# Start of a fused trunk kernel: the first two gate/up pairs come in five contraction parts, the next two in unused SBUF

## The reference

```python
def rms_norm(x, w, eps=NORM_EPS):
    y = xf * lax.rsqrt(jnp.mean(xf * xf, axis=-1, keepdims=True) + eps)
    return (y * w.astype(jnp.float32)).astype(x.dtype)

def swiglu(x, w_gate, w_up, w_down):
    return (jax.nn.silu(x @ w_gate) * (x @ w_up)) @ w_down

h = h + 0.5 * swiglu(rms_norm(h, norm_ff1[i]), ffn1_gate[i], ffn1_up[i], ffn1_down[i])
```

## Time and profile before

| | us |
|---|---|
| median of 3 runs (lowest to highest) | 1050.06 (1049.46 to 1050.34) |
| span of the profiled execution | 1048.1 |
| PE busy in it | 1039.2 (99%) |
| DVE busy | 804.6 (77%) |
| ACT busy | 616.0 (59%) |
| POOL busy | 51.0 (5%) |
| q1 (SP's DMA queue) | 188.79 MB, 63.7% of the 16 engines |

### The profile page before, as it was taken

One profiled execution on the slowest core, in us unless ns is written; L12 is line 12 of the kernel. 1 busy time (PEld: TensorE's weight loads), 2 busy tenths in 40 slices (PEclk: granted clock), 3 DMA queues, 4 the chain that ended last, 5 costly groups with the idle time before them and its releaser, 6 DMA issues.

```text
span 1048.1 us, 18314 instructions
## 1 busy us (share of the span) xinstructions
PE 1039.2 (99%) x6542; PEld 931.7 (89%) x6542; DVE 804.6 (77%) x1192; ACT 616.0 (59%) x979; POOL 51.0 (5%) x70
## 2 busy tenths in 40 slices
PE   9999999999999999999999999999999999999997
PEld 8888888999999988888888888888998998888886
DVE  7888777699768888887766888776689678888663
ACT  7655554478878775555435556543456766556441
POOL 0200012100000000000111000011100000000021
PEclk9999999999999999999999999999999999999999
DMA  9966766559545566666865666676555456667671
GB/s 261 225 189 193 210 195 177 161 152 276 137 120 160 167 197 196 187 195 173 221 182 159 191 193 189 188 219 175 150 166 167 121 156 197 191 192 205 178 205 40
DMA packets 363298, 190.12 MB, mean 181 GB/s; under 512 B 6080, under 2 KB 360672, under 8 KB 363248
## 3 DMA queue, kind: packets, MB, share of 16 engines
q1 hardware_dynamic: 362848, 188.79, 63.7%
q0 software_dynamic: 256, 0.59, 0.3%
q10 hardware_dynamic: 144, 0.10, 0.1%
HBM read 187.86 MB, written 1.07 MB: 180 GB/s over the span
## 4 chain that ended last, share of the span: by engine, by line
PE 95%; DVE 2%; ACT 1%; SPq 1%; issue 1%; DMA 0%; DVEq 0%; ACTq 0%
PE psum L259 46%; PE psum L265 24%; PE psum L240 6%; PE psum L244 6%; PE psum L241 6%; PE psum L1809 1%; PE psum L1814 1%; PE psum L1737 1%; DMA raw<-in_ffn_gate 0%; PE psum L1080 0%; SPq L194 0%; PE psum L1097 0%; DVE xn L355 0%; PE psum L1098 0%; DVE arena L1510 0%
## 5 line engine op out<-in xcount | busy, mean ns | idle before, releaser
L229 DVE TENSOR_TENSOR wlo<-raw,whi 128x1024 fp32r<-128x1024 f32 (+1 forms) x322 | 414.9, 1307 | 68.6 <-ACT whi L224 67.4
L224 ACT ACTIVATE whi<-raw 128x1024 fp32r<-128x1024 f32 (+1 forms) x322 | 351.7, 1113 | 22.7 <-PE psum L244 20.0
L259 PE MATMUL psum<-xn,whi 128*128 128x512 f32 x1392 | 350.4, 393 | 0.4 <-DVE xn L355 0.2
L259 PEld LDWEIGHTS psum<-xn,whi 128*128 128x128 f32 x1392 | 250.6, 189 | 46.2 <-DVE xn L355 1.0
L265 PEld LDWEIGHTS psum<-xn,wlo 128*128 128x128 f32 x1392 | 190.2, 190 | 13.7
L265 PE MATMUL psum<-xn,wlo 128*128 128x256 f32 x1392 | 194.6, 282 | 0.0
L259 PE MATMUL psum<-hid,whi 128*128 128x512 f32 x704 | 171.8, 391 | 0.0
L259 PEld LDWEIGHTS psum<-hid,whi 128*128 128x128 f32 x704 | 128.1, 189 | 24.0
L240 PE MATMUL psum<-xn,whi 128*128 128x256 f32 x416 | 104.5, 289 | 0.0
L241 PE MATMUL psum<-xn,whi 128*128 128x256 f32 x416 | 101.9, 283 | 0.0
L265 PEld LDWEIGHTS psum<-hid,wlo 128*128 128x128 f32 x704 | 92.9, 191 | 4.9
(11 more groups left out here) (248 smaller groups left out, 940.2 us busy)
## 6 DMA issues: line engine op xcount, KB each, us to landing
raw<-in_ffn_down SPq DMA_DIRECT2D x64, 704.0 KB, 4.6
raw<-in_ffn_gate SPq DMA_DIRECT2D x87, 512.0 KB, 3.8
raw<-in_ffn_up SPq DMA_DIRECT2D x87, 512.0 KB, 3.9
raw<-in_hyb_w_in SPq DMA_DIRECT2D x36, 512.0 KB, 4.8
raw<-in_dif_w_qkv SPq DMA_DIRECT2D x24, 512.0 KB, 4.3
raw<-in_hyb_w_out SPq DMA_DIRECT2D x16, 512.0 KB, 4.2
raw<-in_dif_w_o SPq DMA_DIRECT2D x8, 512.0 KB, 3.7
hid<-cs_rows SPq DMA_DIRECT2D x4, 512.0 KB, 7.1
```

Of the source, the lines that this page charges most:

```text
L224: act.activation(whi[:, s, 0:k * P], raw[:, s, 0:k * P], ACT.Copy).then_inc(s_whi, 1)
L229: dve.tensor_tensor(wlo[:, s, 0:k * P], raw[:, s, 0:k * P], whi[:, s, 0:k * P].bitcast(F32), ALU.subtract).then_inc(s_wlo, 1)
L259: mm = pe.matmul(acc, hi[:, j, :], x[:, t, :, :], start=start and j == 0, stop=own and stop and j == k - 1)
```

## The change

The program's first stage is rebuilt; all later stages keep their instructions.

- `PARTS` become (0,1), (1,2), (2,4), (4,6), (6,8) tiles, and each part now holds the tiles of all four blocks 0 to 3 (pairs 0 and 1), as DMAs of one tile of two blocks (128 KB): two per tile, 16 in all.
- SP issues `xT` for the first two parts only; ACT issues the other three itself, behind its first square root.
- Blocks 4 to 7 go to an unused stretch of `arena` (`staged`, four slots) and are split from there; the ring's first loads are blocks 8 to 11, which wait until the last part is split.
- `first_pairs` multiplies each part for all four blocks; in the last part blocks 0 and 1 are finished before blocks 2 and 3. `zero_products` remains twice ahead of part 0, `WARM` becomes 4.
- Pair 2 gets PSUM banks 6 and 7 (`third_parts`). `token_sums` stands behind pair 2 (it stood between the two blocks of pair 1). Pair 3 waits for `s_gu` 2. The PE loop starts with pair 4, and there it waits for `s_gu` 3, which is `merge` of pair 2.
- ACT: squares, splits and corrections of blocks 4 to 7 interleaved, then `token_rms`, then silu and `hidden_hi` of pairs 0 and 1, then the loop with `split_hi` of block 8.
- DVE: `staged_lo(0)`, `merge` of pair 0, `staged_lo(1)`, `merge` of pair 1, two `input_sums`, `staged_lo(2)`, two `input_sums`, `staged_lo(3)`, `token_scale`, the two `normalize`, `product` and `hidden_lo` of both pairs, then `step(2, 0)` with block 8 and `merge` of pair 2.

```diff
-WARM = 5
-PARTS = ((0, 2), (2, 4), (4, 6), (6, 7), (7, 8))
+WARM = 4
+PARTS = ((0, 1), (1, 2), (2, 4), (4, 6), (6, 8))
+STAGED = 9216
+            if isinstance(b, int) and b < 3 * RING:
+                sp.wait_ge(s_wlo, RING)
+            for k in range(k0, k1):
+                for s, w in enumerate((gate, up)):
+                    dst = raw[:, s:RING:2, k * P:(k + 1) * P]
+                    src = w[k * P:(k + 1) * P, 0:2 * P].rearrange("p (b m) -> p b m", b=2)
+                    sp.dma_start(dst, src).then_inc(s_part[i], 16)
+        def staged_hi(act, s):
+            act.wait_ge(s_blk, s + 1)
+            act.wait_ge(s_staged[s], 16)
+            act.activation(whi[:, s, 0:SLOT_IN], staged(s), ACT.Copy).then_inc(s_whi, 1)
+        def staged_lo(dve, s):
+            dve.wait_ge(s_whi, RING + s + 1)
+            dve.tensor_tensor(wlo[:, s, 0:SLOT_IN], staged(s), whi[:, s, 0:SLOT_IN].bitcast(F32),
+                              ALU.subtract).then_inc(s_wlo, 1)
...
@@ ffn_sync, n == 0
-                    load_x(sp, i, k0, k1)
+                    if i < X_BY_SYNC:
+                        load_x(sp, i, k0, k1)
                     load_part(sp, i, gate, up)
-                for s, w in ((2, gate), (3, up)):
-                    load(sp, s, s, w[:, P:2 * P].rearrange("(k p) m -> p k m", p=P), DT)
-                sp.dma_start(con[:, 0:P], a["con"][:, 0:P]).then_inc(s_ones, 16)
-                gate_up(1, True)
+                for s in range(RING):
+                    load_staged(sp, s, (gate, up)[s % 2], 2 * P + (s // 2) * P)
+                    if s == 1:
+                        sp.dma_start(con[:, 0:P], a["con"][:, 0:P]).then_inc(s_ones, 16)
+                gate_up(2)
...
@@ ffn_tensor, n == 0
+                    if i < LAST:
+                        pe.wait_ge(s_phi, i + 1)
+                        rounded(range(RING), tiles)
+                        pe.wait_ge(s_plo, i + 1)
+                        rests(range(RING), tiles)
+                    else:
+                        pe.wait_ge(s_whi, RING)
+                        rounded(range(0, 2), tiles)
+                        pe.wait_ge(s_wlo, RING)
+                        rests(range(0, 2), tiles)
+                        rounded(range(2, RING), tiles)
+                        rests(range(2, RING), tiles)
...
-                first_pair()
-                zero_products(5)
-                gate_up(p0 + 1, 1, before_up=lambda: token_sums(pe, n))
-            with pe.Fori(1, FT // 2) as it:
+                first_pairs()
+                gate_up(p0 + 2, 0, acc=(banks[6], banks[7]))
+                token_sums(pe, n)
+                pe.wait_ge(s_gu, 2)
+                gate_up(p0 + 3, 1)
+            with pe.Fori(1 if n else 2, FT // 2) as it:
...
@@ ffn_scalar, n == 0
+                input_squares(act, 0)
+                input_squares(act, 2)
+                staged_hi(act, 0)
+                corrections(p0, 0)
+                staged_hi(act, 1)
+                corrections(p0 + 1, 1)
+                input_squares(act, 4)
+                input_squares(act, 6)
+                staged_hi(act, 2)
+                staged_hi(act, 3)
                 token_rms(act, n)
+                for g in range(2):
+                    silu(hb + g, g)
+                    hidden_hi(hb + g, g, g)
...
@@ ffn_vector, n == 0
+                staged_lo(dve, 0)
+                merge(p0, hb, 0, True)
+                staged_lo(dve, 1)
+                merge(p0 + 1, hb + 1, 1, True)
                 input_sums(dve, 0)
                 input_sums(dve, 1)
+                staged_lo(dve, 2)
                 input_sums(dve, 2)
                 input_sums(dve, 3)
+                staged_lo(dve, 3)
                 token_scale(dve, n)
+                for g in range(2):
+                    normalize(hb + g, g)
+                for g in range(2):
+                    product(hb + g, g)
+                    hidden_lo(hb + g, g, g)
+                step(2, 0, third_parts)
+                step(2, 1)
...
@@ scalar block, start
+            for i in range(X_BY_SYNC, len(PARTS)):
+                load_x(act, i, *PARTS[i])
```

More of the change, by code:

```diff
@@ L120, in trunk @@
         s_raw = [sem(f"s_raw{i}") for i in range(RING)]
-        s_part = [sem(f"s_part{i}") for i in range(len(PARTS) - 1)]
+        s_staged = [sem(f"s_staged{i}") for i in range(RING)]
+        s_part = [sem(f"s_part{i}") for i in range(len(PARTS))]
         s_dhi = sem("s_dhi")
@@ L175, in tile_of, with load @@
             return buf[:, s, 0:k * P].rearrange("p (k m) -> p k m", k=k)
[L177 to L179 removed]
+        def load(sp, b, s, src, k):
+            if isinstance(b, int) and b < 3 * RING:
+                sp.wait_ge(s_wlo, RING)
+            else:
                 sp.wait_ge(s_wlo, b - RING + 1)
@@ L217, in load_x, with split_hi @@
             sp.dma_start(h[:, tiles, :], a["xT"].rearrange("(d p) t -> p d t", p=P)[:, tiles, :]).then_inc(s_x[i], 16)
[L219 to L223, removed]
+        def split_hi(act, b, s, k, turn):
+            act.wait_ge(s_blk, b - RING + 1)
+            act.wait_ge(s_raw[s], turn * 16 - 16)
             act.activation(whi[:, s, 0:k * P], raw[:, s, 0:k * P], ACT.Copy).then_inc(s_whi, 1)
@@ L554, in zero_products, with first_pairs, rounded, rests @@
                     pe.matmul(banks[7][:, 0:P], rb[:, 0:P], rb[:, 0:P], start=True, stop=True)
-            def first_pair():
-                hi, lo = (part.rearrange("p s (k m) -> p s k m", k=DT) for part in (whi[:, 0:2, 0:SLOT_IN], wlo[:, 0:2, 0:SLOT_IN]))
+            def first_pairs():
+                hi, lo = (buf[:, 0:RING, 0:SLOT_IN].rearrange("p s (k m) -> p s k m", k=DT) for buf in (whi, wlo))
+                def rounded(blocks, tiles):
+                    for b in blocks:
+                        for t in tiles:
+                            pe.wait_ge(s_xlo, t + 1)
+                            pe.matmul(wide(b // 2, b % 2), hi[:, b, t, :], xn[:, t, :, :], start=t == 0, stop=False)
+                def rests(blocks, tiles):
+                    for b in blocks:
+                        for t in tiles:
+                            mm = pe.matmul(wide(b // 2, b % 2)[:, T:2 * T], lo[:, b, t, :], xn[:, t, 0, :], start=False,
+                                           stop=t == DT - 1)
+                        if t == DT - 1:
+                            mm.then_inc(s_blk, 1)
                 for i, (k0, k1) in enumerate(PARTS):
@@ L561, in first_pair @@
                     if i == 0:
[L562 to L565, removed]
+                        pe.wait_ge(s_xhi, 1)
                         zero_products(2)
[L567 to L579, removed]
+                    if i < LAST:
[3 more added lines that the diff above has]
+                        rests(range(RING), tiles)
+                    else:
+                        pe.wait_ge(s_whi, RING)
[4 more added lines that the diff above has]
+                        rests(range(2, RING), tiles)
             if n:
@@ L679, in ffn_vector, with merge @@
             p0, hb = first[n], hidden_before(n)
-            def merge(p, q, g, early=False):
+            def merge(p, q, g, early=False, parts=wide_parts):
                 dve.wait_ge(s_blk, p * 2 + 2)
@@ L686, in merge @@
                 dve.wait_ge(s_cor, q + 1)
-                dve.tensor_tensor(gu[:, g, :, :], wide_parts(g)[0], cor[:, g, :, :], ALU.add).then_inc(s_gu, 1)
+                dve.tensor_tensor(gu[:, g, :, :], parts(g)[0], cor[:, g, :, :], ALU.add).then_inc(s_gu, 1)
             def normalize(q, g):
```

86 lines of the change are left out of this document (30 added, 56 removed).

## The result

| | before | changed |
|---|---|---|
| median (lowest to highest), 4 launches each | 1050.2 (1049.46 to 1050.5) | 1055.92 (1054.19 to 1057.54) |
| ratio, 95% interval | | 1.0057 (1.0045 to 1.0069) |
| span of the profiled execution | 1048.1 | 1052.1 |

The change makes the kernel slower by 5.7 us, where 3.1 was forecast. (Before has four launches here, three in the table ahead of the prediction.) The launches of the changed kernel lie 3.4 us apart, those of before 1.0. Five more launches of it (first experiment) gave 1054.28 in the middle, so its loss is 4.3 to 5.7 us, depending on the set of launches; the middle of all nine is 1055.44.

The account below looks back on a forecast made before the run. PE was taken as the bound; at pair 4, PE alone -0.8, sums wait +1.3, merge wait +2.5, start from idle +0.1 gave a 3.1 us loss. 1050.06 + 3.1 = 1053.2 us, range 1051.2 to 1055.2.

Parts of the forecast that it names:

- The bound and the mechanism: At the start, PE gains by block 3, then waits for DVE and ACT; pair 4 starts at 34.8 against 31.68.
- the sums: PE before the token sums: ready at 24.9, it idles 1.3 us until the last input sums end at 26.2.
- the merge: PE before pair 4: idle 2.5 us until the merge of pair 2 ends at 34.7.
- part 2 as landed once 2.20 MB have passed: Input loading: at the rates seen before, part 2 lands at 9.7 us and PE has it at 10.8.
- the upper bound of 10.75: Latest landing of part 2, when before's last part landed behind the same 2.20 MB; carries through to 1054.3 us.
- an order kinder to SP: Input loading: SP's queue served ahead of ACT's would bring part 2 earlier than 9.7, at 8.4 at the earliest.
- the chain of DVE and ACT: From block 0's end at 17.85: 8.3 us to the token sums; from their end 7.9 to pair 2's merge at 34.7.
- rival (c): TensorE's clock falls in the gaps between parts and the later ones, costing 2 us: 1055.2 us; chance 0.12.
- the table load: Silu table load on ACT after the root, 1.28 us: costed at nothing, over 0.6 us before normalize.
- the loads of blocks 4 to 11: Blocks 4 to 7 land by 20 us and cost nothing; ring loads issue near 16, block 8 not wanted before 31.
- (a): Part 2 at 8.4 to 9 and a chain shorter by half a microsecond or more: loss 0.5 to 2 us, about 1051.5; chance 0.18.
- (b): DVE and ACT do not hold PE at pair 4; PE's own sum decides: 1049.3 us, down to 1047.3; chance 0.06.

Follow-up runs that it names:

- first experiment: The changed kernel launched five more times with no edit: 1054.28 us (1054.16 to 1055.5).
- The experiment with the early sums: Changed kernel with squares and sums ahead of block 4's split, token sums ahead of pair 2, token scale and silu worked in earlier: 1051.61 us.
- the one with the removed wait: Changed kernel with pair 4 not waiting for the merge of pair 2, pair 5 still waiting for that of pair 3: 1054.33 us.
- the kernel with the hold: Changed kernel with SP waiting for part 2 to land before it issues part 3, launched twice: 1057.97 and 1056.36 us.
- the second trace: Profiled launch of the changed kernel run again with no edit: 1055.44 us, span 1053.4.
- the kernel with filled parts: Changed kernel with products of zeros put back: 6 instead of 4 at the start, 3 behind part 0 and 3 behind part 1: 1055.98 us.
- the first trace: Profiled launch of the changed kernel from its first four launches, no further edit: 1054.19 us, span 1052.1.
- both kernels with the late gaps filled: Unread products, 3 before the token sums and 8 before pair 4, in the changed kernel: 1054.28 us; also with all input issued by SP: 1054.3.

## Why the prediction was right and where it was wrong

**The bound and the mechanism: right.** All of the loss sits at pair 4, and PE has its two new waits where they were put: 1.1 us for the sums (1.3 forecast) and 2.5 us for the merge (2.5). Counted from block 3's end the merge of pair 2 ends 15.5 us later (35.44 - 19.92); forecast was 15.4 (34.7 - 19.3). The experiment with the early sums took the chain's part away and with it 2.6 us; the one with the removed wait showed that the wait only passes the chain on.

**The data: the term that was mis-sized.** The step "part 2 as landed once 2.20 MB have passed", 9.7, failed. With the input on two queues it landed at 10.2 to 10.8 in six traces and at 11.5 to 11.6 in two, and the upper bound of 10.75, taken from before's last part, was too low. The runs show two things in its place. Bytes that passed are not a DMA that is complete: 98% had passed at 9.0, the last one was done at 10.2 (the kernel with the hold). And it matters that ACT issues part of the input: with one queue part 2 was copied at 9.6 to 10.1, with two at 10.3 to 11.6. I had counted the second issuer as neutral for bandwidth and allowed only for an order kinder to SP; the order was worse for it, for part 0 above all (0.5 to 2.3 us later). How much of this is the mixing and how much the 0.52 MB less ahead of part 2 is open. This term is worth 0.6 us in the profiled launch and 1.9 in one like the second trace.

**The landing term by launches.** Put into the forecast's own sum, part 2 ready at 11.39 to 12.7 instead of 10.8 gives pair 4 at 35.4 to 36.7 and a time of 1053.8 to 1055.1. Measured at pair 4: 35.57 to 36.88. The other 0.2 us in both is the chain of DVE and ACT, 0.1 us longer than forecast (17.0 against 16.9 from block 0's end), and rounding. The range of the data was taken from one trace and used as the range of the launches. The landing alone thus brings a launch to the end of the range: that of the second trace took 1055.44, 0.2 beyond it.

**The clock, rival (c): partly right.** It was priced at 2 us and put between the parts as much as in the late gaps. In the parts the half level did occur (part 0 of the profiled launch; granted clock 0.50 from 8 to 10 us in the second trace) but beside a wait for data, and filling these gaps did not help. Behind the 2.5 us gap it cost 1.3 us in one trace and 1.5 in two, and nothing in three, among them the change's own two. By the Trainium skill ("TensorE: Matmul & The Clock Gate", "Part 1: The HAM clock gate") idleness takes the full clock back. The three traces with a loss agree; the other three kept the full clock over the same gap. For the change itself a fallen clock behind the gap is argued and not shown. The 3.4 us between its four launches are more than the 1.3 us that late data alone made between its two traces. Their mean granted clocks fit only roughly: 0.998, 0.995, 0.997 and 0.995 at 1054.19, 1057.54, 1055.98 and 1055.87 us. Only the fastest of the four has a trace.

**The range** ended at 1055.2, the value of rival (c) alone. Late data (part 2 copied at 11.51) and a fallen clock (1.3 us) did come in the same launch, that of the kernel with filled parts, which took 1056.66. I had let the cases exclude each other. Luck has a part in the miss as well: the middle of the first four launches, 1055.92, lies outside the range, that of the next five, 1054.28, inside.

**Costed at nothing, and rightly:** the table load (over 0.65 us early), the removed fillers (1050.06 against 1050.0 in the kernel before), and the loads of blocks 4 to 11. Rivals (a) and (b), a small loss and a gain, had no part in any launch of the change.

## What to carry to other kernels

Before giving a starving engine more work early, follow the other engines' chain from the last of that work to the next wait of that engine: here PE was 0.2 us ahead of before (19.92 + 0.43 + 11.17 = 31.5 against 31.68) and ran into 3.6 us of new waits, because the sums, the scale and the splits lost their cover. Read the slack of that wait in the kernel before (0.74 us here): a chain that comes later by more than the slack becomes the bound. And give a landing the time of its DMA, from issue to landing in a loaded queue, and a spread over launches, not the moment at which its bytes have passed. Where a gap on PE may or may not cost the clock, add that cost to the other late cases and do not set it beside them.

## What the runs showed of the hardware

- With 0.79 MB of the input on ACT's queue beside SP's, SP's small DMAs came later and less steadily. The third one, 128 KB issued at 1.69 us, landed 4.3 to 5.9 us later in eight traces; with all on one queue 3.6 to 3.8 in three.
- With two queues a DMA can be overtaken: one issued at 5.33 landed at 11.6, the next two on its queue, issued at 6.09 and 6.81, at 10.3 and 10.8. In the kernel with filled parts it was the same (5.50 to 11.5; 6.39 and 6.91 to 10.4 and 10.9). In the three traces with one queue the 16 weight DMAs landed in the order of their issue.
- The last of the bytes take long: 98% of 2.20 MB had passed at 9.0 us, all of it was complete at 10.2.
- A gap of 2.51 us on PE was followed by products at full level in three traces and at half level in three (1.3 to 1.5 us lost). Two launches of one program gave one of each, 1.6 us apart.
- The table's granted clock reads 1.00 over 6 to 10 us of the first trace, where 4 wide products took 2.07 us instead of 1.17: there the pitch of the products shows the level, the table's figure does not.
- The time from the first product of pair 4 to the end of the span is 1016.4 to 1016.5 us in six traces without a fallen clock (before, the change twice, both kernels with the late gaps filled, one with the hold). The rest of a millisecond reproduces to 0.1 us there; once, in the kernel with all input on SP, another 0.5 us was lost in the last products.
